# Routing in three parts, block numbers by rounding, one-hot pairs beside their products, a residual in halves

## What is computed

```python
x = layer_norm(ALPHA * x + (1.0 + gate) * mixed, ln_g[layer, 0], ln_b[layer, 0])
h = x * (1.0 + scale) + shift
...
scores = jax.nn.sigmoid((t @ router_w).astype(f32))
grouped = (scores + router_bias.astype(f32)).reshape(T, N_GROUPS, EXPERTS_PER_GROUP)
group_score = lax.top_k(grouped, GROUP_SCORE_TOP)[0].sum(-1)
best = jnp.argmax(group_score, axis=-1)
in_group = grouped[jnp.arange(T), best]
_, local = lax.top_k(in_group, TOP_K)
gates = jnp.take_along_axis(scores, experts, axis=1)
...
dest = pad_start[sorted_e] + jnp.arange(A) - start[sorted_e]
row_tok = jnp.zeros((P,), jnp.int32).at[dest].set((order // TOP_K).astype(jnp.int32))
```

## Time and profile before

| | us |
|---|---|
| median of three runs | 3673.89 (3673.41 to 3682.86) |
| the profiled execution | 3682.2 |
| its span | 3680.4 |
| busy: TensorE, VectorE, ScalarE, GpSimd | 3143.7, 2013.3, 1218.9, 508.4 |
| `route_idx` written, layer 0 and layer 1 | 2007.3 and 3177.7 |

### The profile page before, as it was taken

One profiled execution on the slowest core, in us unless ns is written; L12 is line 12 of the kernel. 1 busy time (PEld: TensorE's weight loads), 2 busy tenths in 40 slices (PEclk: granted clock), 3 DMA queues, 4 the chain that ended last, 5 costly groups with the idle time before them and its releaser, 6 DMA issues. The chain is left out here.

```text
span 3680.4 us, 41343 instructions
## 1 busy us (share of the span) xinstructions
PE 3143.7 (85%) x14464; PEld 1974.9 (54%) x14464; DVE 2013.3 (55%) x4016; ACT 1218.9 (33%) x2938; POOL 508.4 (14%) x553
## 2 busy tenths in 40 slices
PE   8999999589999996996894999959978699499970
PEld 4555555378888885995453444424434245244430
DVE  3886685399999954885775000045346334400008
ACT  1112222245544433663662122212256423122212
POOL 0000100100000002211000111011068600000001
PEclk9999999689999987998896999979989899699995
DMA  7453233511011102223532999963133442499976
GB/s 261 154 197 102 65 123 114 185 35 36 29 36 38 36 15 86 96 81 131 193 128 86 334 366 363 328 235 132 69 106 106 119 147 84 145 359 363 365 286 211
DMA packets 364861, 583.98 MB, mean 159 GB/s; under 512 B 54518, under 2 KB 259830, under 8 KB 364426
## 3 DMA queue, kind: packets, MB, share of 16 engines
q1 hardware_dynamic: 295560, 361.43, 30.0%
q0 software_dynamic: 31312, 110.26, 8.5%
q10 hardware_dynamic: 37812, 109.99, 7.7%
HBM read 456.94 MB, written 124.68 MB: 158 GB/s over the span
## 5 line engine op out<-in xcount | busy, mean ns | idle before, releaser
L364 PE MATMUL inp__bank<-inp__hT,inp__w 128*128 128x512 f32 (+1 forms) x1536 | 559.5, 523 | 1.0 <-DVE inp__hT L508 1.0
L2610 PE MATMUL moe__bank<-moe__wgu,moe__xT 128*128 128x512 f32 x1024 | 457.3, 600 | 15.5 <-DMA moe__wgu<-in_moe_w_up_dram 13.9
L364 PEld LDWEIGHTS inp__bank<-inp__hT,inp__w 128*128 128x128 f32 x1536 | 289.2, 190 | 254.3 <-issue 239.5
L2115 PE MATMUL close__bank<-close__w_out,close__catT 128*128 128x512 f32 x640 | 285.3, 600 | 42.5 <-DMA close__w_out<-in_at_w_out_dram 32.5
L2610 PEld LDWEIGHTS moe__bank<-moe__wgu,moe__xT 128*128 128x128 f32 x1024 | 191.4, 192 | 237.5 <-issue 224.6
L2728 DVE TENSOR_TENSOR moe__hid<-moe__sg,moe__bank 128x256 f32<-128x256 f32 x64 | 27.0, 421 | 486.7 <-ACT moe__sg L2671 486.7
L2627 PE MATMUL moe__bank<-moe__wdn,moe__hidT 128*128 128x512 f32 x512 | 230.5, 593 | 2.9 <-ACT moe__hidT L2675 2.9
L2115 PEld LDWEIGHTS close__bank<-close__w_out,close__catT 128*128 128x128 f32 x640 | 121.0, 193 | 188.5 <-issue 174.9
L3010 PE MATMUL cq__bank<-cq__w,cq__hT 128*128 128x512 f32 x480 | 212.3, 599 | 11.4 <-DMA cq__w<-in_at_w_in_dram 11.4
L3382 POOL TENSOR_SCALAR attn__p<-attn__p,attn__rec 128x384 f32<-128x384 f32 x160 | 196.0, 1248 | 93.4 <-DVE attn__rec L3357 93.4
L433 ACT ACTIVATE inp__z<-inp__bank 128x512 f32<-128x512 f32 (+1 forms) x96 | 50.5, 526 | 404.8 <-PE inp__bank L364 404.8
(11 more groups left out here) (458 smaller groups left out, 5868.3 us busy)
## 6 DMA issues: line engine op xcount, KB each, us to landing
moe__wdn<-in_moe_w_down_dram ACTq DMA_DIRECT2D x64, 1024.0 KB, 8.5
moe__wgu<-in_moe_w_gate_dram SPq DMA_DIRECT2D x64, 1024.0 KB, 7.4
moe__wgu<-in_moe_w_up_dram SPq DMA_DIRECT2D x64, 1024.0 KB, 14.7
inp__wv<-in_ada_w_dram SPq DMA_DIRECT2D x10, 4096.0 KB, 16.0
scratch_y_rows<-moe__y ACTq DMA_DIRECT2D x64, 512.0 KB, 8.9
scratch_zt<-inp__tb SPq DMA_DIRECT2D x32, 640.0 KB, 4.9
inp__w<-in_ab_w_in_dram POOLq DMA_DIRECT2D x31, 512.0 KB, 4.8
rwkv__rk<-scratch_zt SPq DMA_DIRECT2D x20, 512.0 KB, 3.9
```

Of the source, the lines that this page charges most:

```text
L364: mm = pe.matmul(zbank[j][g][:, 0:n], w[:, j, k, :], hT[:, k, t0:t0 + n], start=k == 0, stop=k == KC - 1)
L2115: mm = pe.matmul(bank[2 + c][:], catT[:, i % (3 if layer else 2), k, :], w_out[:, k, c * 512:(c + 1) * 512], start=k == 0, stop=k == KC - 1)
L2610: mm = pe.matmul(bank[2 + j][:], xT[:, j, k, :], wgu[:, j, k].rearrange("p a n -> p (a n)"), start=k == 0, stop=k == KC - 1)
```

## The change

- `route` takes a part and a stage; parts are tiles 0 to 5, 6 to 8 and 9. Stage 0 waits for the part's exponential and goes up to the picked group's scores, stages 1 and 2 choose the first and the second expert, and stage 2 also sums. Stage 0 of part 0 stands at the end of VectorE's step 8, stages 1 and 2 at the end of step 9; parts 1 and 2 stand behind the loop. ScalarE takes the exponential of part 0 in step 7 ahead of `shifted`, that of part 1 in step 10, that of part 2 at the end.
- The residual's add and statistics are done by halves of 512 columns, the first half ahead of the wait for the second half's projection; `x2_r` counts two per tile.
- The block number is the place times 1/128 plus a constant, rounded by adding and taking away 1.5 * 2^23. The one-hot pair of each of the 20 columns of `dest` is made by two tensor_scalar instructions, and TensorE's product of a column waits for its pair alone.
- The expert bases move up, and a compare and a product become one instruction.

```diff
-    EARLY = NT - 1
+    PARTS = ((0, 6), (6, 9), (9, NT))
+    MAGIC = 1.5 * 2 ** 23
...
-                        sp.wait_ge(x2_r, i - 2)
+                        sp.wait_ge(x2_r, 2 * (i - 2))
...
-                pe.wait_ge(hot_r, 1)
                 for n in range(2 * NT):
+                    pe.wait_ge(hot_r, 2 * n + 2)
                     mm = pe.matmul(bank[1][:, 0:BLOCKS], at_pos[:, n, :], in_blk[:, n, :], start=n == 0, stop=n == 2 * NT - 1)
...
+                def exp_logits(part):
+                    lo, hi = PARTS[part]
+                    act.wait_ge(lg, hi)
+                    act.activation(sc[:, 0, lo * E:hi * E], bank[6][:, lo * E:hi * E], ACT.Exp, scale=-1.0).then_inc(sg, 1)
...
                     if s == NT:
-                        act.wait_ge(lg, EARLY)
-                        act.activation(sc[:, 0, 0:EARLY * E], bank[6][:, 0:EARLY * E], ACT.Exp, scale=-1.0).then_inc(sg, 1)
+                        exp_logits(1)
...
+                        if s == 7:
+                            exp_logits(0)
                         shifted(s - 1)
-                act.wait_ge(lg, NT)
-                act.activation(sc[:, 0, EARLY * E:W], bank[6][:, EARLY * E:W], ACT.Exp, scale=-1.0).then_inc(sg, 1)
+                exp_logits(2)
...
-                    dve.wait_ge(taken, 2 * i + 2)
-                    dve.wait_ge(x_l[r], 16 * (i // 3) + 16)
-                    dve.scalar_tensor_tensor(x2[:], x[:, r], ALPHA, x2[:], ALU.mult, ALU.add).then_inc(x2_r, 1)
-                    dve.wait_ge(x2_r, i + 1)
-                    for c in range(2):
-                        clink(dve.bn_stats(stats[:, c], x2[:, c * 512:(c + 1) * 512]))
+                        if c == 0:
+                            dve.wait_ge(x_l[r], 16 * (i // 3) + 16)
+                        dve.wait_ge(taken, 2 * i + c + 1)
+                        dve.scalar_tensor_tensor(x2[:, cols], x[:, r, cols], ALPHA, x2[:, cols], ALU.mult, ALU.add).then_inc(x2_r, 1)
+                        dve.wait_ge(x2_r, 2 * i + c + 1)
+                        clink(dve.bn_stats(stats[:, c], x2[:, cols]))
...
-                dve.wait_ge(router_l, 48)
-                link(dve.memset(upto[:, 0], 0.0))
-                route(0, 0, EARLY)
-                route(1, EARLY, NT)
+                    if s == 8:
+                        dve.wait_ge(router_l, 48)
+                        link(dve.memset(upto[:, 0], 0.0))
+                        route(0, 0)
+                    if s == 9:
+                        route(0, 1)
+                        route(0, 2)
+                for part in (1, 2):
+                    for stage in range(3):
+                        route(part, stage)
                 dve.sem_inc(pos_in, 1)
                 more = link
+                base = cmp[:, BLOCKS - 1]
+                more(dve.tensor_scalar(base, rank[:, 0:E], float(P), None, ALU.mult))
...
-                more(dve.tensor_scalar(upto[:, 0:TILES], place[:, 0:TILES], float(P), None, ALU.is_ge))
-                more(dve.tensor_tensor(upto[:, 0:TILES], upto[:, 0:TILES], nb[:, 3].unsqueeze(1).broadcast_to([P, TILES, E]), ALU.mult))
+                more(dve.scalar_tensor_tensor(upto[:, 0:TILES], place[:, 0:TILES], float(P), nb[:, 3].unsqueeze(1).broadcast_to([P, TILES, E]),
+                                              ALU.is_ge, ALU.mult))
...
-                more(dve.tensor_tensor(past, places.unsqueeze(2).broadcast_to([P, 2 * NT, BLOCKS + 1]),
-                                       cf[:, CONST["steps"]].unsqueeze(1).broadcast_to([P, 2 * NT, BLOCKS + 1]), ALU.is_ge))
-                more(dve.tensor_tensor(in_blk[:], past[:, :, 0:BLOCKS], past[:, :, 1:BLOCKS + 1], ALU.subtract))
-                more(dve.tensor_reduce(lane[:, 0], past[:, :, 1:BLOCKS + 1], AX.X, ALU.add))
+                more(dve.tensor_scalar(lane[:, 0], places, 1.0 / P, -127.0 / 256.0, ALU.mult, ALU.add))
+                more(dve.tensor_scalar(lane[:, 0], lane[:, 0], MAGIC, None, ALU.add))
+                more(dve.tensor_scalar(lane[:, 0], lane[:, 0], -MAGIC, None, ALU.add))
                 more(dve.scalar_tensor_tensor(lane[:, 1], lane[:, 0], -float(P), places, ALU.mult, ALU.add))
-                more(dve.tensor_tensor(at_pos[:], lane[:, 1].unsqueeze(2).broadcast_to([P, 2 * NT, P]),
-                                       cf[:, CONST["lane"]].unsqueeze(1).broadcast_to([P, 2 * NT, P]), ALU.is_equal))
-                for c in range(2):
-                    more(dve.tensor_tensor(in_blk[:, NT * c:NT * c + NT], in_blk[:, NT * c:NT * c + NT], per_head(tok[:], BLOCKS), ALU.mult))
-                dve.sem_inc(hot_r, 1)
+                for n in range(2 * NT):
+                    dve.tensor_scalar(in_blk[:, n], rank[:, 0:BLOCKS], lane[:, 0, n:n + 1], tok[:, n % NT:n % NT + 1],
+                                      ALU.is_equal, ALU.mult).then_inc(hot_r, 1)
+                    dve.tensor_scalar(at_pos[:, n], cf[:, CONST["lane"]], lane[:, 1, n:n + 1], None, ALU.is_equal).then_inc(hot_r, 1)
```

More of the change, by code:

```diff
@@ L2370, in columns, with route @@
                     link(dve.tensor_scalar(grow[:], grow[:], 1.0, None, ALU.add))
-                def route(part, lo, hi):
-                    dve.wait_ge(sg, part + 1)
+                def route(part, stage):
+                    lo, hi = PARTS[part]
                     nt = hi - lo
@@ L2382, in route @@
                     m0, m1, m2, m3 = (r1[:, n, lo:hi] for n in range(4))
-                    link(dve.tensor_scalar(s0, s0, 1.0, None, ALU.add))
-                    link(dve.reciprocal(s0, s0))
-                    link(dve.tensor_tensor(by_tile(s1, E), by_tile(s0, E), rb[:].unsqueeze(1).broadcast_to([P, nt, E]), ALU.add))
-                    g4 = s1.rearrange("p (g e) -> p g e", e=PER)
-                    pairs = [(e1, e2) for e1 in range(PER) for e2 in range(e1 + 1, PER)]
-                    for n, (e1, e2) in enumerate(pairs):
-                        ins = dve.tensor_tensor(r6[:, n, wg], g4[:, :, e1], g4[:, :, e2], ALU.add)
@@ L2409, in route @@
+                    if stage > 0:
+                        c = stage - 1
                         chosen, weight = r4[:, 2 + c, wp], r4[:, 5, wp]
@@ L2423, in route @@
                                                by_tile(chosen, PER).unsqueeze(2).broadcast_to([P, nt, GROUPS, PER]), ALU.mult))
-                    link(dve.tensor_tensor(place[:, lo:hi], one[:, 0, lo:hi], one[:, 1, lo:hi], ALU.add))
-                    for t in range(lo, hi):
-                        link(dve.tensor_tensor(upto[:, t + 1], upto[:, t], place[:, t], ALU.add))
+                    if stage == 2:
+                        link(dve.tensor_tensor(place[:, lo:hi], one[:, 0, lo:hi], one[:, 1, lo:hi], ALU.add))
+                        for t in range(lo, hi):
+                            link(dve.tensor_tensor(upto[:, t + 1], upto[:, t], place[:, t], ALU.add))
                 means(0)
@@ L2473, in _ @@
                 more(dve.tensor_scalar(nb[:, 3], nb[:, 3], float(E - 1), float(P), ALU.add, ALU.mult))
[L2474 to L2475 removed]
+                more(dve.scalar_tensor_tensor(upto[:, 0:TILES], place[:, 0:TILES], float(P), nb[:, 3].unsqueeze(1).broadcast_to([P, TILES, E]),
+                                              ALU.is_ge, ALU.mult))
                 more(dve.tensor_tensor(place[:, 0:TILES], place[:, 0:TILES], upto[:, 0:TILES], ALU.add))
[L2477 to L2478 removed]
+                more(dve.tensor_tensor(place[:, 0:TILES], place[:, 0:TILES], base.unsqueeze(1).broadcast_to([P, TILES, E]), ALU.add))
                 for c in range(2):
@@ L2502, in _ @@
                 dve.wait_ge(idx_mm, 1)
-                more(dve.tensor_scalar(past[:, 0, 0:BLOCKS], bank[1][:, 0:BLOCKS], 0.25, None, ALU.add))
-                more(dve.tensor_copy(idx[:], past[:, 0, 0:BLOCKS]))
+                more(dve.tensor_scalar(in_blk[:, 0], bank[1][:, 0:BLOCKS], 0.25, None, ALU.add))
+                more(dve.tensor_copy(idx[:], in_blk[:, 0]))
             @block.gpsimd
```

45 lines of the change are left out of this document (25 added, 20 removed).

## The result

| | before | after |
|---|---|---|
| median of five runs, us | 3677.86 (3673.41 to 3682.86) | 3653.17 (3640.45 to 3658.72) |
| ratio | | 0.993, 95% interval 0.9911 to 0.9949 |
| the profiled execution, its span | 3682.2, 3680.4 | 3640.45, 3638.7 |
| layer 0: closing loop, tail | 183.70, 58.76 | 185.51, 46.24 |
| layer 1: closing loop, tail | 168.36, 58.79 | 168.40, 45.94 |

The kernel is 0.7% faster. The two layers together took 469.6 us before and 446.1 after, 23.5 us less.

A forecast was written before the change was run, and what follows sets the result against it. VectorE was taken to set the tail between closing loop and experts. Routing 7.0, position arithmetic 2 x 0.42 and pairs 2 x 4.6 summed to 17.1 us, giving 3656.8 us; range 3650 to 3666.

The forecast's parts named there:

- The sum: Whole kernel: routing 7.0, position arithmetic 2 x 0.42 and one-hot pairs 2 x 4.6 us gained, 17.1 us together.
- Layer 1 of the routing: Part 0 fits layer 1's loop with 1.0 us to spare; part 2 starts 5.12 us earlier.
- Layer 0 of the routing: Part 0 doesn't fit layer 0's loop: TensorE stalls 1.9 us ahead of tile 9's projection, 1.9 us gained.
- The rival that it would lower the clock: Layer 0's stall slows tile 9's projection by 3.5 us, 3660.3 at most; chance 0.13 together with a moved loop end.
- The added table switches: ScalarE's added loads cost 1.28 us each; rival with 1.38 us drain per switch: 4.7 us stall in layer 0, chance 0.05.
- The pairs: Block numbers to index copy: one-hot pairs beside TensorE's products take 12.75 us instead of 17.35, 4.6 gained per layer.
- 0.47 a pair: VectorE's two tensor_scalar instructions, 0.294 and 0.334 us less 0.08 overlap each; 9.4 us for 20 pairs.
- the rival without overlap: VectorE's one-hot instructions don't overlap: 0.63 us a pair, gain 10.6 us in all, 3663.3; chance 0.12.
- The rival of broken overlap on TensorE: Waits between pairs make TensorE's loads and products run end to end, 14 us more per layer, 3694; chance 0.04.
- The position arithmetic: VectorE's tail: base moved ahead of a wait and compare fused with multiply, 0.42 us gained per layer.
- part 2 starts at 3137.37 where it started at 3142.49: Layer 1's tail: last tile's routing starts right behind ScalarE's last exponential, 5.12 us earlier.

The follow-up runs named there:

- e5: Changed kernel plus a one-column Sqrt and Exp behind ScalarE's shifted tile 6, so two more tables are loaded; one run 3670.58 us.
- e0: The changed kernel measured again with no edit; 3660.45 us, ratio 0.9957.
- e2: Changed kernel with block numbers and one-hots made in whole instructions as before, one wait ahead of the products; 3670.18 us, ratio 0.9972.
- b1: The kernel before the change run again with no edit, for a second profile; one run 3676.36 us.
- e3: Changed kernel with the residual's add whole over 1024 columns behind the second half, as before; 3649.59 us, ratio 0.9923.
- e9: Changed kernel with part 0's exponential ahead of catT's copies and the block list on GpSimd, measured a second time; 3654.54 us, ratio 0.9933.
- e4: Changed kernel with TensorE waiting for all 20 one-hot pairs ahead of its first product; one run 3670.23 us.
- e8: The changed kernel measured once more with no edit; 3652.6 us, ratio 0.9927.
- e6: Changed kernel with part 0's exponential ahead of catT's copies and the root's table loaded right behind it; 3659.72 us, ratio 0.995.
- e7: Changed kernel with part 0's exponential ahead of catT's copies and the block list moved from VectorE to GpSimd; 3657.23 us, ratio 0.9942.

## Why the prediction was right, and where it wasn't

**The sum.** 17.1 us were forecast, and 17.9, 25.0 and 24.7 came out in three measurements. The time of 3656.8 stood on a median of 3673.89 for the kernel before, which came out at 3677.86 over five runs. That it lies 3.6 us from the measured 3653.17 is luck in part: the gain of 24.7 was 7.6 us larger than forecast, and the base 4.0 us too low. The two layers alone give 18.0 to 23.5 us.

**Layer 1 of the routing: right.** Stage 0 with its memset took 3069.65 to 3076.36, 6.71 us for 6.70 forecast; the bank came free 1.06 us ahead of the need, for 1.0. Part 1 took 3102.62 to 3111.88, 9.26 for 9.26. A straight line between two measured sizes was enough for a chain of small instructions. e5 showed the spare time from the other side, where 3.0 us more of ScalarE's work became 1.93 of stall.

**Layer 0 of the routing: right, at full clock.** The stall was 2.12 us for 1.9 forecast. The rival that it would lower the clock came true in two of six executions with this stall (e0, e2) and cost 1.7 us, half of the 3.5 that it was priced at. With it, moving part 0 earned nothing in layer 0 of e0; without it, 1.8 to 3.9 us, where 1.9 was forecast. Nor need a gap be that long: behind 1.88 to 1.92 us the projection of tile 1 was slower by the same 1.7 us in b1, e3 and e9.

**The added table switches: no drain.** The Exp row stands 1.29 us behind the start of its load and the root's 1.30, as in the earlier trace rows, and in e5 two switches more made the stalls 3.0 and 1.93 us longer. The Trainium skill (ScalarE: Activation LUTs, What ACT_TABLE_LOAD costs) gives 1283 ns for the load, with which the rows agree, and about 1380 ns of drain with each switch, of which these rows show nothing. By an estimate from that figure of the page, e5's two switches would have made the stalls some 2.8 us longer than the 5.14 and 1.93 that were measured; for a switch between two activations of this kernel the measurement decides.

**The pairs: right mechanism, wrong size.** The term "0.47 a pair" measured 0.413. The forecast took both instructions' lengths from a line fitted to 256 and 512 columns with two pointers; `in_blk`, 52 columns, came out at 0.302 for 0.294, but `at_pos`, with one pointer, at 0.278 for 0.334 at 128 columns. Whether the missing pointer makes that difference wasn't tried. From the block numbers to the copy it was 11.62 for 12.75: 5.7 us per layer gained instead of 4.6, and 2.3 more in all. The overlap of 0.08 was right (0.08 to 0.09), so the rival without overlap falls. The rival of broken overlap on TensorE falls by the products' 8.77 us, and e4 puts the gain down to the products that run beside.

**The position arithmetic: a little more.** From the last `upto` instruction to the first block number it was 10.41 us and is 9.84 (3118.85 to 3128.69): 0.57 for 0.42 per layer.

**What was left out: the clock in the tail.** The step "part 2 starts at 3137.37 where it started at 3142.49" took the chain of the last tile at the speed that it had in the one profiled execution. The tail then lies on that chain, and the chain on a clock that differs from one execution to the next: the wait for the last exponential was 1.12 in that working, and 0 to 2.67 us in the runs. Nothing was costed for it, though the router took 3.59, 3.40, 3.18 and 2.64 us in the one trace of before. For the 5.12 us that part 2 was to start earlier in layer 1, counted from the end of the last projection, the three executions have 6.5 (after), 5.5 (e0) and 4.0 (e8).

**The terms as measured**, for e0, with the forecast in brackets: part 2 starts 3.9 and 5.5 us earlier behind the last projection and the loops are 3.9 longer (3.8 of it the stall and the slower projection), so 5.4 for the routing (7.0); 1.2 for the position arithmetic (0.84); 11.4 for the pairs (9.2). That is 18.0, for 17.1. In e8 it is 6.1 + 1.1 + 11.4 = 18.6 (two loops 3.4 longer), in the profiled after 10.9 + 1.2 + 11.4 = 23.5. So in e0 and e8 the total is near the forecast because a routing that earned 0.9 to 1.6 us less and pairs that earned 2.3 more stood against each other, which is luck; in after nothing stood against. The rest of its 41.7 us lies in phases that the change doesn't touch.

**Open:** why the clock falls behind one gap of 2.1 us and not behind another of the same length in the same kernel; whether the 2.1 us of e6 hold in the time; and why VectorE's instructions take longer beside those of GpSimd in e7. That needs more runs than were made.

## What to carry to other kernels

Where one engine makes many operands at once and another consumes them in order, making them one by one beside the consumer can pay even when the making itself gets slower: here 0.8 us dearer and 6.5 us better covered. Work moved from a tail into a loop is free only up to the next engine's need, and that is read by two starts, when the buffer is wanted and when the moved step ends; each us beyond is paid, and a stall can cost a lower clock on top. After a tail is shortened, look at which chain sets it now, since what had slack before, such as a product behind a gap, then shows in the time. And work given to an idle engine isn't free for the others: in e7 GpSimd took over 2.3 us of VectorE's instructions, and VectorE lost 2.1 us beside it.

## What the runs showed of the hardware

- The same 16 router passes behind the same 2.99 us gap took 1.97 to 3.62 us, and the same projection behind a 2.12 us gap 7.10 or 8.80 us (granted clock 1.00 or 0.61 in a window behind it), in one and the same kernel. In two executions of the kernel before, 32 passes took 14.00 us behind a gap of 1.28 and 15.70 behind one of 1.88. A gap's cost in clock can't be read from one execution.
- tensor_scalar with per-partition pointers, back to back with an increment each: 0.302 us at 52 columns with two pointers, 0.278 at 128 columns with one, neighbours overlapping by 0.08 to 0.09.
- GpSimd made the block list in about 7 us (3142.33 to 3149.36 in e7) beside VectorE; on VectorE its five instructions take 2.3. Meanwhile four VectorE instructions took 1.15, 0.89, 1.03 and 0.59 us that take 0.19, 0.49, 0.49 and 0.49 in e6, and it is the same in both layers of e7 and of e9.
